# Five classes of experts instead of three, one slot table, alternating heavy and light experts, and rebuilt edges between the stages of a decoder layer

## The chip, the cores and the metric

The kernel runs on one core of one Trainium2 chip. The metric is the device time of one execution in microseconds (us). Lower is better.

## The reference

One layer of a hybrid decoder is computed for 1024 prompt tokens and 8 sample tokens (1032 in all, width 1024, everything in float32). Cut to what matters:

```
h = rms_norm(x);  q_lat | kv_lat | k_rope | conv_in | q_mem | gates = h @ w_in
y_a = latent attention (8 heads);  y_b = conv branch (GLU, depthwise conv of width 31, LayerNorm, silu)
y_c = cross-attention into 256 memory tokens (their keys and values come from rms_norm(mem) @ w_mem_kv)
x = x + (sig(g_a) * y_a + sig(g_b) * y_b + sig(g_c) * y_c) @ w_out
h = rms_norm(x)
scores = sigmoid(h @ w_router);  top 8 of 64 experts by scores + b_router, weights = scores / sum * 2.5
x = x + sum over chosen experts e of weight * (silu(h @ w_gate[e]) * (h @ w_up[e])) @ w_down[e]
      + (silu(h @ w_s_gate) * (h @ w_s_up)) @ w_s_down                        # shared expert
```

An expert has two matrices of 1024 x 256 and one of 256 x 1024, 3 MB in all. 1032 tokens with 8 choices each are 8256 (token, expert) pairs over 64 experts, 129 to an expert on average; the counts differ from expert to expert.

## The kernel before

The kernel is a row of stages with a barrier of all engines after each: `stage_constants`, `stage_front` (memory keys and values, normalised tokens), `stage_tokens` (prompt attention), `stage_sample` (sample attention), `stage_merge` (gates, branch projections, conv), `stage_mixer` (output projection, router, slot records, shared expert) and `stage_experts`. Inside a stage every engine has its own instruction stream, written out by hand, and waits on semaphores. SP issues most loads, and POOL issues the indirect transfers. Each engine works strictly in order.

**Constants and front.** `stage_constants` loads three tables and waits for them. `stage_front` then loads 11 row tiles; for each, ACT squares, POOL takes the root, DVE normalises, and PE transposes. DVE waits first for three small gain vectors (`gains_in`), one of them broadcast over the partitions (`gk`). PE works the memory projections in between, and at the end DVE normalises the memory keys.

**Merge.** PE makes gate columns (`gate`) and branch columns (`out`, needs the attention output `oT`) in units of 344 tokens; ACT takes sigmoids; DVE multiplies them (`merge`) and between them works 124 steps of the convolution (`conv`), 1024 columns each. POOL issues the loads of `oT` (`branch_in`) after the conv state has landed. Two banks hold the branch units, so PE can be at most two units ahead of DVE.

**Mixer.** For each of nine row tiles (the ninth is the 8 samples) PE projects with `w_out` (`project`), transposes the normalised rows (`turn`), makes router scores (`route`), and counts places (`rank`); DVE adds, normalises, takes the top 8 (`choose`), and works out the place of each slot record (`prefix`, `place`); POOL scatters the records (token and weight) to a table in DRAM. Six units of the shared expert (`shared`) fill PE at the end. `rank_experts` sorts the experts by count, so that rank 0 is the fullest.

**Experts.** Each rank has a fixed number of slots, its cap: `RANK_CAPS = ((192, 12), (160, 28), (128, 24))`. If a count is above the cap, the whole loop runs a second time over the next slots (`passes`). The experts are worked in order of rank. For an expert:

- SP loads the three matrices four experts ahead (`load`, rings of 4).
- POOL gathers the token rows as quarter rows, one indirect transfer for each 32 slots (`gather`, L2418), three experts ahead.
- DVE transposes them 32 x 32 (`turn`, L2524).
- PE multiplies gate and up (`gate_up`, L2612): 32 matmuls, moving columns = cap. ACT takes silu, DVE multiplies (`gate`, L2530).
- PE multiplies down (`down`): L2622 for the first 128 slots, L2630 for the tail (the slots beyond 128) in 2 or 4 column groups of the array.
- ACT (and DVE for half of the tail) scale the result by the slot weight into `yb`, two buffers.
- POOL adds the rows to the sums in DRAM by an indirect accumulating transfer: L2438 for the 128 rows, L2445 for the tail. Before each L2438 POOL waits until the adds of the expert before have landed (`added`), since two adds may touch the same row. The gathers three experts ahead stand before this wait in POOL's stream.

At the start of the loop PE also computes the down product of the shared expert (L2649), DVE adds it to x (L2542), and ACT stores the sums that the experts add to. After the loop SP copies the sums to the outputs.

Of the kernel before, what the change touches and what calls it, by code (L numbers as in the profile page):

```python
# [95 lines left out]
def stage_constants(nc, a, keep):  # L96

    with Core(nc) as c:
        loaded = c.sem("constants_loaded")
        cleared = c.sem("buffers_cleared")  # L100
        with c.block() as block:
            @block.sync
            def _(sp):
                sp.dma_start(keep.ident[:, :], a["k_ident"]).then_inc(loaded, 16)
                sp.dma_start(keep.cos[:, :, :], a["k_cos"].rearrange("(t p) c -> p t c", p=P)).then_inc(loaded, 16)
                sp.dma_start(keep.sin[:, :, :], a["k_sin"].rearrange("(t p) c -> p t c", p=P)).then_inc(loaded, 16)

                sp.wait_ge(loaded, 48)

            @block.gpsimd  # L110
            def _(pool):
                pool.memset(keep.mhalf[:, :], -0.5).then_inc(cleared, 1)
                pool.wait_ge(cleared, 1)


def stage_front(nc, a, o, keep):
# [4 lines left out]
    with Core(nc) as c:  # L121
# [19 lines left out]
        S = {n: c.sem("p_" + n) for n in """gains_in k_w_in v_w_in next_in squares mean rsq h_ready h_psum hT_ready k_psum v_psum k_out v_ready  # L141
# [20 lines left out]
        with c.block() as block:  # L162
            @block.sync
            def _(sp):
# [9 lines left out]
                rows(0)  # L174
                for dst, name in ((g_mem, "g_mem_norm"), (g_attn, "g_attn_norm")):
                    sp.dma_start(dst[:, :], a[name][0].rearrange("(k p) -> p k", p=P), allow_slow_non_contiguous=True).then_inc(S["gains_in"], 16)
                sp.dma_start(gk[:, :], a["g_k_mem"][0].partition_broadcast(P)).then_inc(S["gains_in"], 16)
# [7 lines left out]
                for j in range(9, ROWS_TILES):  # L185
                    rows(j)
                w_lat, w_qm, w_uq, w_uk, w_uv = keep.token_weights
# [15 lines left out]
                sp.wait_ge(S["next_in"], 112)  # L203
# [21 lines left out]
            def _(pool):  # L225
                for j in range(ROWS_TILES):
# [7 lines left out]
            def _(v):  # L234
# [16 lines left out]
                v.wait_ge(S["gains_in"], 48)  # L251
# [7 lines left out]
                v.wait_ge(S["k_out"], NMEM)  # L259
                v.tensor_tensor(kn[:, :], k[:, :], k[:, :], ALU.mult).then_inc(S["k_step"], 1)  # L260
                v.wait_ge(S["k_step"], 1)
                v.tensor_reduce(ssk[:, :], kn3, AX.X, ALU.add).then_inc(S["k_step"], 1)
                v.wait_ge(S["k_step"], 2)
                v.tensor_scalar(mnk[:, :], ssk[:, :], 1.0 / MHD, EPS, ALU.mult, ALU.add).then_inc(S["k_mean"], 1)
                v.wait_ge(S["k_rsq"], 1)
                v.tensor_tensor(kn3, k3, spread(rsk[:, :], MHD, 2), ALU.mult).then_inc(S["k_step"], 1)
                v.wait_ge(S["k_step"], 3)
                v.tensor_tensor(kn3, kn3, spread(gk[:, :], NMEM * MH), ALU.mult).then_inc(S["k_ready"], 1)

            @block.tensor  # L270
            def _(pe):
# [15 lines left out]

                for j in range(5):
                    turn(j)
# [1267 lines left out]
def stage_merge(nc, a, o, keep):  # L1557
# [8 lines left out]
    with Core(nc) as c:  # L1566
# [26 lines left out]
            last_psum last_ready stored state_moved""".split()}  # L1593
# [10 lines left out]
        with c.block() as block:  # L1604
            @block.sync
            def _(sp):
# [17 lines left out]

                def gated_rows(i):
# [6 lines left out]
                sp.dma_start(state, a["state_conv"][0].rearrange("(g b) r c -> (b r) g c", g=2)).then_inc(S["state_in"], 16)  # L1632
                gated_rows(0)
                weights(0, 0)
                weights(1, 0)
                for i in range(1, KC):
                    gated_rows(i)
                weights(2, 0)
                weights(3, 0)
                sp.dma_start(o["conv_s"][:, 0:HIST - 1, :], a["state_conv"][0][:, 1:HIST, :]).then_inc(S["state_moved"], 16)  # L1640
                for b in range(4, KD):
                    weights(b, 0)
# [1125 lines left out]
```

## Time and profile before

| | |
|---|---|
| median of 3 runs | 2620.87 us (2620.84 to 2622.55) |
| the profiled execution | 2621.16 us, its span 2619.3 us |
| PE busy | 2487.0 us (95%) |
| DVE, ACT, POOL busy | 1044.1, 594.9, 786.2 us |
| mean granted TensorE clock | 0.983 |
| bytes moved | 406.88 MB, 155 GB/s over the span |

The span is the time from the first to the last instruction. PE is TensorE's matmul stream, PEld its weight loads, DVE VectorE, ACT ScalarE, POOL GpSimd, SP SyncE; a q behind an engine's name is its sequencer, which issues transfers. A PE row counts two records for one float32 matmul. The stages in the trace: front to about 65 us, merge from 1116 to 1487, mixer from 1489 to 1717, experts from 1717 to the end.

### The profile page before, as it was taken

What the parts mean: (1) busy time and instruction counts of PE and PEld (TensorE: products, weight loads), DVE (VectorE), ACT (ScalarE), POOL (GpSimd) and SP (SyncE); (2) the same over time, 40 slices, a digit from 0 to 9 for tenths busy, and PEclk for the clock granted to TensorE, in tenths of its full rate; (3) what the DMA queues carried; (4) which work ended last, traced back from release to release, by engine and by line L of the source; (5) the groups of instructions that cost most, each with busy time, mean ns of one, the idle gap of its engine ahead of it and who ended that gap; (6) DMA issues with size and microseconds to landing.
All of it is one profiled execution on the core that took longest, in us unless ns stands there. A gap on an engine that the chain in (4) does not pass through costs nothing. (4 is left out here: it accounts for less than half of the span.)

```text
span 2619.3 us, 35201 instructions
## 1 busy us (share of the span) xinstructions
PE 2487.0 (95%) x12240; PEld 1665.7 (64%) x12240; DVE 1044.1 (40%) x2287; ACT 594.9 (23%) x1177; POOL 786.2 (30%) x590
## 2 busy tenths in 40 slices
PE   6999999999899999989999899889999999999995
PEld 3566666665645555556666655547777777787774
DVE  3223334544434444169952246433233333322220
ACT  2222333333233434110021111101112221121111
POOL 1000000000035455210000025435555666655542
PEclk9999999999899999999999999999999999999998
DMA  7111111010242221171112341077999999999996
GB/s 266 48 42 43 43 43 40 30 38 25 76 111 81 80 80 51 36 212 45 37 54 62 106 158 50 1 263 247 287 293 329 329 327 323 324 340 365 369 367 193
DMA packets 206451, 406.88 MB, mean 155 GB/s; under 512 B 55915, under 2 KB 135072, under 8 KB 189804
## 3 DMA queue, kind: packets, MB, share of 16 engines
q1 hardware_dynamic: 168884, 314.39, 34.9%
q0 software_dynamic: 29856, 78.51, 12.0%
q10 hardware_dynamic: 7536, 11.73, 1.2%
q8 instruction: 100, 1.64, 0.3%
q14 instruction: 75, 0.61, 0.1%
HBM read 343.53 MB, written 72.83 MB: 159 GB/s over the span
## 5 line engine op out<-in xcount | busy, mean ns | idle before, releaser
L2418 POOL DMA_INDIRECT mergedT<-tokens_normed,gather_rows x308 | 313.1, 1017 | 121.7 <-issue 96.6
L2612 PEld LDWEIGHTS pGe<-xT,we_g 128*128 128x128 f32 x2048 | 272.7, 191 | 46.6 <-issue 24.2
L2612 PE MATMUL pGe<-xT,we_g 128*128 128x160 f32 (+2 forms) x2048 | 286.0, 298 | 9.1 <-DVE xT L2524 9.0
L2612 PE MATMUL pUe<-xT,we_u 128*128 128x160 f32 (+2 forms) x2048 | 280.3, 295 | 0.0
L2612 PEld LDWEIGHTS pUe<-xT,we_u 128*128 128x128 f32 x2048 | 273.6, 191 | 0.0
L2524 DVE STREAM_TRANSPOSE xT<-mergedT 128x1280 f32<-128x1280 f32 (+2 forms) x64 | 154.3, 2412 | 266.0 <-DMA mergedT<-tokens_normed,gather_rows 266.0
L1403 PE MATMUL pKs<-ws_uk,cTs 128*128 128x512 f32 x512 | 234.4, 600 | 1.2 <-issue 1.2
L1116 POOL TENSOR_TENSOR rk<-ssk,half 128x32 f32<-128x32 f32 x32 | 173.3, 5427 | 191.7 <-DVE ssk L1245 191.7
L2622 PE MATMUL pYe<-we_d,h_e 128*128 128x512 f32 x512 | 230.1, 593 | 0.0
L2438 POOL DMA_INDIRECT sums<-mergedT,add_rows x64 | 103.9, 1624 | 269.5 <-issue 97.7
L2478 ACT ACTIVATE mergedT<-pYe,wc 128x512 f32<-128x512 f32 x128 | 88.0, 687 | 414.7 <-PE pYe L2622 414.7
L1313 DVE TENSOR_REDUCE ssk<-sqs 128x8 f32<-128x512 f32 x128 | 87.6, 684 | 210.4 <-ACT sqs L1179 210.1
L1727 DVE SCALAR_TENSOR_TENSOR y_conv<-hist,taps,y_conv 128x1024 f32<-128x1024 f32 x120 | 154.0, 1283 | 3.4
L1403 PEld LDWEIGHTS pKs<-ws_uk,cTs 128*128 128x128 f32 x512 | 92.5, 191 | 98.1 <-issue 97.1
L2622 PEld LDWEIGHTS pYe<-we_d,h_e 128*128 128x128 f32 x512 | 93.8, 191 | 92.2 <-issue 92.2
L1795 PE MATMUL pGate<-hT,branch_w 128*128 128x344 f32 x480 | 143.7, 453 | 0.0
L2221 PE MATMUL pXf<-w_out,mergedT 128*128 128x512 f32 (+2 forms) x320 | 128.9, 560 | 7.5 <-DMA w_out<-in_w_out 7.5
L1803 PE MATMUL pBranch<-oT,branch_w 128*128 128x344 f32 x384 | 120.1, 466 | 11.7 <-DMA oT<-attention_out 6.4
L499 POOL TENSOR_TENSOR r<-n,minus_half 128x16 f32<-128x16 f32 x9 | 26.1, 2899 | 328.5 <-DVE n L685 328.5
L808 PE MATMUL pFill<-hT,fill_w 128*128 128x344 f32 x384 | 119.9, 456 | 4.6 <-ACT fill_out L517 4.5
L808 PE MATMUL pFill<-hT,first_w 128*128 128x344 f32 x384 | 119.6, 457 | 2.5 <-ACT fill_out L517 2.5
L1795 PEld LDWEIGHTS pGate<-hT,branch_w 128*128 128x128 f32 x480 | 91.3, 190 | 47.3
(422 smaller groups left out, 3259.1 us busy)
## 6 DMA issues: line engine op xcount, KB each, us to landing
we_g<-in_w_e_gate SPq DMA_DIRECT2D x64, 1024.0 KB, 7.1
we_u<-in_w_e_up SPq DMA_DIRECT2D x64, 1024.0 KB, 11.7
we_d<-in_w_e_down SPq DMA_DIRECT2D x64, 1024.0 KB, 16.3
mergedT<-in_cache_latent SPq DMA_DIRECT2D x96, 128.0 KB, 2.1
raw_columns<-fill_out SPq DMA_DIRECT2D x48, 172.0 KB, 1.8
first_w<-in_w_in SPq DMA_DIRECT2D x12, 512.0 KB, 5.2
branch_w<-in_w_in SPq DMA_DIRECT2D x10, 512.0 KB, 4.8
mergedT<-tokens_normed,gather_rows POOLq DMA_INDIRECT x308
```

What stands on the lines that cost most here:

```text
L808: mm = pe.matmul(pG[:, 0:GN], ring[b % 2][:, k, :], keep.hT[:, k, g * GN:(g + 1) * GN], start=k == 0, stop=k == KD - 1)
L1116: pool.tensor_tensor(rk[b % 2][:, :, g, :], ssk[b % 2][:, :, g, :], half[:, :].rearrange("p (j h) -> p j h", h=NHEAD), ALU.pow).then_inc(S ...
L1403: mm = pe.matmul(pK[n % 2][:, :], cT[b % 2][:, k, n * P:(n + 1) * P], w_uk[:, k, :], start=k == 0, stop=k == KL - 1)
L1727: v.scalar_tensor_tensor(y[:, i, 0:SEQ], hist[:, i, j:j + SEQ], taps[:, i, j:j + 1], y[:, i, 0:SEQ], ALU.mult, ALU.add).then_inc(S["tap"], 1)
L1795: pe.matmul(pG[g][:, 0:n], ring[b % W][:, 4 + k, :] if b else keep.first_w[:, k, :], keep.hT[:, k, at:at + n], start=k == 0, stop=k == KD - 1)
L1803: mm = pe.matmul(pY[u % 2][:, 0:n], ring[b % W][:, k, :], branch[:, k, at:at + n], start=k == 0, stop=k == 3)
L2221: mm = pe.matmul(pX[p][0:r, at:at + n], keep.mergedT[:, k, cols_of(t)], w_out[:, k, at:at + n], start=k == 0, stop=k == KD - 1)
L2418: pool.indirect_dma_start(out=xg[v % 2][:, g, :], out_offset=None, in_=quarter, in_offset=bass.IndirectOffsetOnAxis(ap=gi[v % W][:, g:g + ...
L2438: pool.indirect_dma_start(out=keep.acc_dram[:, :], out_offset=bass.IndirectOffsetOnAxis(ap=si[u % W][:, 0:1], axis=0), in_=yb[u % 2][:, 0, ...
L2524: v.transpose(xT[p][:, :, 0:n * GR].rearrange("p c (g i) -> p g c i", g=n), xg[p][:, 0:n, :].rearrange("p g (j c) -> p g c j", c=KD)).then ...
L2612: mm = pe.matmul(dst[p][:, f * CAP:f * CAP + n], w[r][:, k, f * P:(f + 1) * P], xT[p][:, k, 0:n], start=k == 0, stop=k == KD - 1)
L2622: mm = pe.matmul(pY[half][:, :], h[p][:, f, 0:P], wd[r][:, f, half * 512:(half + 1) * 512], start=f == 0, stop=f == 1)
```

## The change

- `stage_constants` is gone. Its identity table is loaded in `stage_front` behind the first row tile, its cos and sin tables late in that stage, and `gk` after the row tiles with a semaphore of its own. DVE normalises the memory keys before it takes the last two transposed tiles.
- Merge: `branch_in` moves from POOL to SP. Its first half stands behind the weights of block 0 and the first raw conv rows; the other raw rows come between weight loads. ACT does the sigmoid of the first conv rows before the taps, DVE does 8 conv steps ahead of the first unit instead of 6, and the first 128 columns of `w_out` are loaded into `first_w` near the end of the stage.
- Mixer: the projection of tiles 0 and 1 begins with these 128 columns. The samples are projected in four column groups at once (`project_samples`). Shared units 0 to 3 stand between the last tiles' steps, and `rank(NTT - 2)` comes after `shared(2)`. `rank_experts` has five classes.
- Experts: `RANK_CAPS` has five classes, a pass is 128 slots further on, one table serves all classes, and the 28 experts of the lowest class are spread among the other 36. The first `turn` comes after the additions of seven tiles instead of five. At the end `down` of expert 62 comes before `gate_up` of expert 63, and silu and gate of 63 behind the scaling of 62.

```
-RANK_CAPS = ((192, 12), (160, 28), (128, 24))
-PASSES = max(-(-min(TOK, TOK * TOPK // (sum(n for _, n in RANK_CAPS[:i]) + 1)) // c) for i, (c, _) in enumerate(RANK_CAPS))
+RANK_CAPS = ((192, 4), (176, 8), (160, 8), (144, 16), (128, 28))
+PASSES = max(1 - (c - min(TOK, TOK * TOPK // (sum(n for _, n in RANK_CAPS[:i]) + 1))) // P for i, (c, _) in enumerate(RANK_CAPS))
+GT = P // GR * (PASSES - 1) + NG_E
...
-                    marks.mark(v.tensor_scalar(over[:, :], thr[0:NE, :], low, count, ALU.mult, ALU.is_lt))
+                    marks.mark(v.tensor_scalar(over[:, :], thr[0:NE, :], low, count, ALU.add, ALU.is_lt))
...
+    LIGHT = RANK_CAPS[-1][1]
+    ranks = {False: iter(range(NE - LIGHT)), True: iter(range(NE - LIGHT, NE))}
+    RANK_AT = [next(ranks[(u + 1) * LIGHT // NE > u * LIGHT // NE]) for u in range(NE)]
+    CAPS = [[c for c, n in RANK_CAPS for _ in range(n)][rank] for rank in RANK_AT]
+    GROUPS = [-(-c // GR) for c in CAPS]
...
-                                mm = pe.matmul(pZ[c * n:(c + 1) * n, 0:D // parts], h[p][:, f, P:P + n], wd[r][:, f, part(c, parts)], start=f == 0, stop=f == 1)
+                                mm = pe.matmul(pZ[P // parts * c:P // parts * c + n, 0:D // parts], h[p][:, f, P:P + n], wd[r][:, f, part(c, parts)], start=f == 0, stop=f == 1)
...
+                def project_samples():
+                    p = NT % 2
+                    pe.wait_ge(S["x2_ready"], NT - 1)
+                    for k in range(KD):
+                        for q in range(4):
+                            out = pX[p][32 * q:32 * q + DB, 0:256]
+                            x_k = keep.mergedT[:, k, SEQ:TOK]
+                            if q:
+                                mm = pe.matmul(out, x_k, w_out[:, k, q * 256 - P:(q + 1) * 256 - P], start=k == 0, stop=k == KD - 1)
+                            else:
+                                pe.matmul(out[:, 0:P], x_k, keep.first_w[:, k, :], start=k == 0, stop=k == KD - 1)
+                                pe.matmul(pX[p][0:DB, 512:512 + P], x_k, w_out[:, k, 0:P], start=k == 0, stop=k == KD - 1)
...
-                route(NTT - 1)
-                shared(1)
+                shared(2)
+                rank(NTT - 2)
+                route(NTT - 1)
+                shared(3)
...
-                pool.wait_ge(S["state_in"], 16)
-                branch_in(0)
```

## Rows read from the trace of the kernel before

**Rows 1.** Windows of the experts' loop: length, busy us by engine, clock, DMA share, GB/s.

```profile
1760.00:1945.00 185.00, 185.00 (x945) 145.99 (x944) 57.45 (x99) 27.86 (x44) 95.98 (x84) 1.00 0.86 280
1945.00:2340.00 395.00, 395.00 (x2616) 312.54 (x2613) 130.25 (x209) 80.39 (x146) 236.57 (x204) 1.00 1.01 326
2340.00:2562.00 222.00, 213.71 (x1439) 171.80 (x1438) 48.42 (x98) 35.14 (x60) 111.05 (x99) 1.00 1.03 364
```

**Rows 2.** Chain of waits, caps of 192, then of 160: start us, us, what.

```profile
1913.74 5.40 PE pGe L2612 x32
1924.34 3.43 PE pYe L2622 x8
1927.77 1.87 PE pZe L2630 x8
...
2039.68 4.54 PE pGe L2612 x32
...
2052.01 1.00 PE pZe L2630 x16
```

**Rows 3.** Timeline, an expert of cap 128: start us, us, engine, line, what.

```profile
2441.45 3.84 PE L2612 MATMUL pGe<-xT,we_g 128*128 128x128 f32 x32 [0.68 <-DVE xT L2524]
...
2448.70 3.60 PE L2622 MATMUL pYe<-we_d,h_e 128*128 128x512 f32 x8
```

**Rows 4.** Chain of waits later in the loop, the indirect adds.

```profile
2082.52 10.98 DMA sums<-mergedT,add_rows
...
2336.34 10.09 DMA sums<-mergedT,add_rows
...
2549.89 9.99 DMA sums<-mergedT,add_rows
```

**Rows 5.** The first adds (L2438) alone, landing time: 1780 to 1940, then 2340 to 2562.

```profile
DMA to landing us min/median/max: 8.4/10.8/11.7
...
DMA to landing us min/median/max: 10.0/10.1/10.9
```

**Rows 6.** Timeline, the front.

```profile
7.57 0.34 SPq L172 DMA_DIRECT2D mem_x<-in_mem_prompt  x1
15.89 0.15 DVE L238 TENSOR_SCALAR front_mean<-front_ss 128x1 f32<-128x1 f32 x1 [15.89 <-DMA mem_gk<-in_g_k_mem]
```

**Rows 7.** Timeline, the merge.

```profile
1132.66 1.23 DVE L1738 TENSOR_TENSOR hist<-convT,y_conv 128x1024 f32<-128x1024 f32 x1 [19.78 <-ACT y_conv L1676]
1140.55 8.84 PE L1803 MATMUL pBranch<-oT,branch_w 128*128 128x344 f32 x24 [6.35 <-DMA oT<-attention_out]
1145.42 0.51 DVE L1748 TENSOR_TENSOR mergedT<-gate_sig,pBranch 128x344 f32<-128x344 f32 x1 [3.91 <-ACT gate_sig L1694]
1305.40 4.93 PE L1803 MATMUL pBranch<-oT,branch_w 128*128 128x344 f32 x8 [4.77 <-DVE gated L1752]
```

**Rows 8.** Timeline, the mixer.

```profile
1494.63 29.87 PE L2221 MATMUL pXf<-w_out,mergedT 128*128 128x256 f32 x96 [7.45 <-DMA w_out<-in_w_out]
1626.31 7.03 PE L2221 MATMUL pXf<-w_out,mergedT 128*8 128x512 f32 x16
1652.91 0.69 PE L2251 MATMUL pCf<-chosen,before 128*128 128x64 f32 x2 [6.52 <-DVE chosen L2100]
1653.81 7.56 PE L2264 MATMUL pXf<-mergedT,w_sg 128*128 128x344 f32 x16
1661.21 4.79 PE L2264 MATMUL pXf<-mergedT,w_su 128*128 128x344 f32 x16
```

**Rows 9.** Timeline, the start of the experts' stage.

```profile
1751.25 3.76 PE L2649 MATMUL pZe<-w_sd,shared_hT 128*128 128x512 f32 x4 [6.06 <-DVE mergedT L2542]
1760.19 5.47 PE L2612 MATMUL pGe<-xT,we_g 128*128 128x192 f32 x32
```

**Rows 10.** Timeline, the end.

```profile
2584.01 7.03 PE L2622 MATMUL pYe<-we_d,h_e 128*128 128x512 f32 x16
2596.53 1.57 POOL L2438 DMA_INDIRECT sums<-mergedT,add_rows  x1 [5.77 <-DMA sums<-mergedT,add_rows]
```

More of the change, by code:

```diff
@@ L1929, in stage_mixer @@
         pR, pC = c.ps("pRf"), c.ps("pCf")
-        w_out_in = [c.sem(f"f_w_out_in{part}") for part in range(4)]
+        w_out_in = [c.sem(f"f_w_out_in{part}") for part in range(3)]
+        PARTS = ((P, 384), (384, 640), (640, D))
         x_in = [c.sem(f"f_x_in{p}") for p in range(2)]
@@ L1955, in x_load @@
                     sp.dma_start(x[t % 2][0:rows_of(t), :], src).then_inc(x_in[t % 2], 16)
-                for part in range(4):
-                    sp.dma_start(w_out[:, :, part * 256:(part + 1) * 256],
-                                 a["w_out"][0].rearrange("(k p) n -> p k n", p=P)[:, :, part * 256:(part + 1) * 256]).then_inc(w_out_in[part], 16)
+                for part, (at, end) in enumerate(PARTS):
+                    sp.dma_start(w_out[:, :, at - P:end - P], a["w_out"][0].rearrange("(k p) n -> p k n", p=P)[:, :, at:end]).then_inc(w_out_in[part], 16)
                 x_load(0)
@@ L2215, in project @@
                         pe.wait_ge(S["x2_ready"], t - 1)
-                    n = 512 if t else 256
-                    for at in range(half * 512, (half + 1) * 512, n):
-                        pe.wait_ge(w_out_in[at // 256], 16)
-                        pe.wait_ge(w_out_in[(at + n) // 256 - 1], 16)
+                    for at, end in pieces:
+                        for part, (first, past) in enumerate(PARTS):
+                            if at < past and first < end:
+                                pe.wait_ge(w_out_in[part], 16)
                         for k in range(KD):
-                            mm = pe.matmul(pX[p][0:r, at:at + n], keep.mergedT[:, k, cols_of(t)], w_out[:, k, at:at + n], start=k == 0, stop=k == KD - 1)
-                    if half:
+                            w = w_out[:, k, at - P:end - P] if at else keep.first_w[:, k, :]
+                            mm = pe.matmul(pX[p][0:r, at:end], keep.mergedT[:, k, cols_of(t)], w, start=k == 0, stop=k == KD - 1)
+                    if end == D:
                         mm.then_inc(S["x2_psum"], 1)
+                def project_samples():
[10 more added lines that the diff above has]
+                                pe.matmul(pX[p][0:DB, 512:512 + P], x_k, w_out[:, k, 0:P], start=k == 0, stop=k == KD - 1)
+                    mm.then_inc(S["x2_psum"], 1)
                 def turn(t):
@@ L2294, in stage_experts @@
     CQ = D // 4
-    CAPS = [c for c, n in RANK_CAPS for _ in range(n)]
-    NGS = sorted({c // GR for c in CAPS}, reverse=True)
+    LIGHT = RANK_CAPS[-1][1]
[3 more added lines that the diff above has]
+    GROUPS = [-(-c // GR) for c in CAPS]
+    RANK_CLASS = {c: i for i, (c, _) in enumerate(RANK_CAPS)}
     TAILS = sum(c > P for c in CAPS)
```

277 lines of the change are left out of this document (150 added, 127 removed).

## The prediction

> **What bounds the kernel now.** I read the slices of the page first: PE is busy in nine tenths of nearly every slice, so the first question is what work PE is given, and the second where its few pauses lie. For the experts' loop I then asked for windows [rows 1]: PE is busy for all of 1760 to 2340 and for 213.71 of the last 222 us, and at the same time the transfer engines are full, at 326 to 364 GB/s. The chain of waits shows which of the two ends last. Under cap 192 it is all PE, and an expert takes 15.90 us from its gate matmuls to the end of its tail (1913.74 to 1929.64); under cap 160 it is 13.33 us (2039.68 to 2053.01) [rows 2]. Later in the loop the chain runs through the indirect adds instead [rows 4]. From 2082.52 to 2336.34 it makes 19 steps, 13.36 us each, which is PE's own pace. From 2336.34 to 2549.89 it makes 19 steps of 11.24 us, where PE needs only 10.68: 7.25 us for gate and up [rows 3] and 3.43 for down [rows 2]. So there are two bounds close together: PE's work by cap, and POOL's rule that one expert's adds land before the next expert's start. An add takes about 10.1 us to land [rows 4, 5], so the next follows 1.1 us later; an expert with a tail has two adds, one behind the other, and takes 2.1 us more (13.36 less 11.24). The other stages are PE's, with pauses at the edges [rows 6 to 9]. After a pause PE is slow as well: 7.56 us for what takes 4.79 right behind it [rows 8].
>
> **The loop.** One step of 16 slots is half the difference between two caps. Gate and up take 15.90 - 3.43 - 1.87 = 10.60 us under cap 192 and 13.33 - 3.43 - 1.00 = 8.90 under 160 [rows 2], and 7.25 under 128 [rows 3]: 0.85 and 0.82 us a step. The tail of cap 176 keeps the two column groups of 512 columns (1.87), that of 144 the four groups of 256 (1.00), since the moving side is the same. So cap 176 takes 15.05 and cap 144 takes 12.50.
>
> - Before: 12 x 15.90 + 28 x 13.33 + 24 x 10.68 = 820.4 us. Measured, from the first gate matmul at 1760.19 [rows 9] to the last down at 2591.04 [rows 10], it is 830.9: the 10.5 more are mostly the light experts' wait for the adds (19 x 0.56 = 10.6 by rows 3 and 4).
> - After: 4 x 15.90 + 8 x 15.05 + 8 x 13.33 + 16 x 12.50 + 28 x 10.68 = 789.7 us.
>
> Now the second bound. Experts with a tail need about 13.3 us in the chain of adds (13.36 was PE-paced), light ones 11.24. With seven light to nine heavy, a heavy expert and its share of 0.78 light ones take: under 192 and 176, PE 24.2 and 23.4 against 22.1 in the chain, no loss; under 160, PE 21.7 against 22.1, a loss of 0.4; under 144, PE 20.8 against 22.1, a loss of 1.3. That is 8 x 0.4 + 16 x 1.3 = 24 us. Two things take from it. The adds may lag behind PE by some 5 us before the gathers, which stand behind them on POOL, come late; and a tail of 16 rows instead of 32 should land a little sooner, for which I take 0.2 us for 16 experts, 3 us. So the loss is 16 us, the loop 806, the gain 25. The ends of the loss are 0 (the chain never binds) and 27 us (neither lag nor shorter tails, and a few landings like the 10.98 of rows 4), so the gain lies between 14 and 41. By the caps there are 304 gathers against 308, and the weight loads stay. The extra DVE copy of a heavy expert lies in DVE's idle time (130 us busy of 395, rows 1).
>
> A rule of the Trainium skill bears on this. The first adds land in 10.8 us where the engines move 280 GB/s and in 10.1 us where they move 364 [rows 1, 5]. The page "DMA: Bandwidth & Descriptors" (Latency and other measured facts) says that lighter memory load makes the fixed cost of a transfer smaller. By that rule the mixed order would shorten the landings, since no stretch stays at 364 GB/s, and rival A would come; the trace has the opposite sign, so I leave its chance at 0.2.
>
> **The front.** The first row tile is requested at 7.57 us [rows 6], behind the constants block; now it is the first request, 6.8 us earlier. DVE's first step waited for the broadcast gains until 15.89, which is also gone, so behind it the loads of tiles and of memory weights are what is late. At the end the key stores leave before the last product: about 1 us. Gain 8, bounds 5 (loads take over) and 10.
>
> **The merge.** PE's wait of 6.35 us for `oT` goes, with about 1.9 us of slow clock: 24 records of 344 columns took 8.84, and by the 3.43 us for 8 of 512 [rows 2] they need 6.9 [rows 7]. SP's queue then holds 1.8 MB ahead of `oT` (state, weights, raw rows) and 2.1 MB of it; at the 326 GB/s of rows 1 that is 12 us from the stage's start at 1116, so it lands by about 1130, before PE asks at 1134.2 (1140.55 - 6.35). But DVE is next: at 1305.40 PE waits 4.77 us for it [rows 7], which then was behind with its conv steps. DVE starts about 3 us earlier (1132.66), loses the 3.91 us wait before 1145.42, and has two more conv steps of 1.3 us there: 3 + 3.9 - 2.6 = 4.3, and with part of the slow clock 5. Bounds 0 (ACT stuck behind the raw rows, which now hold up the taps) and 9 (DVE not binding).
>
> **The mixer.** PE's wait for `w_out` of 7.45 us [rows 8] takes in two projections of 128 columns, 16 matmuls, 3.84 us at full clock [rows 3]; I take 4.5, since part of the slow clock behind the wait falls into it too. A rule speaks against part of it: the page "TensorE: Matmul & The Clock Gate" (What's actually happening) says that the array starts at 1.2 GHz after idling. By it these projections take 7.7 us, which is more than the whole wait, and gain 3 at most; rows 8 show the same slowness behind the wait of 6.52. The samples cost two times 7.03 us [rows 8]; in four column groups 8 matmuls of 256 columns took 1.00 us [rows 2], and here are 32 such and 8 halves more: 4.0 to 4.9, against 14.1 if the groups do not overlap. I take 4.7: gain 9.4. The wait of 6.52 us before rank(7) goes behind shared(2), with the slow clock after it (7.56 - 4.79 = 2.8, and 0.6 in the rank products): 9.9. Splitting each projection at column 128 costs 0.2 us for 8 tiles, 1.5. The longer `rank_experts` (four classes more, about 2 us of small steps) lies under shared units 4 and 5, twice 4.79 us each [rows 8]; without this cover it would cost its 2 us. What is late next are the last tile's records on POOL: PE has only these two units, 19 us, left behind rank(8), and I expect both to end together. Sum 22, bounds 13 and 25.
>
> **Start and end of the experts.** PE waits 6.06 us for an addition that stands behind `turn` on DVE, and then runs slowly (3.76 for 4 records, half of the 3.43 for 8 in rows 2 is 1.7) [rows 9]. After the change the 16 records that are left at 1745.2 (1751.25 - 6.06) follow at once, 6.9 us, and PE reaches the first gate matmul at about 1752.1 instead of 1760.2; the one table costs 4 small DVE copies more, 0.5. Gain 7.5, bounds 3 and 9. At the end the last add waits 5.77 us for the one before [rows 10]. With expert 62's down first, that add starts 10.7 us earlier (7.25 + 3.43), and the last one follows the last product by about 2 us instead of 5.5 (2596.53 - 2591.04); PE now waits about 1 us for gate(63). Gain 2.5, bounds 0 and 5.
>
> **Sum.** 25 + 8 + 5 + 22 + 7.5 + 2.5 = 70 us against the profiled execution: 2621.16 - 70 = 2551.2. The median of the runs is 0.3 lower, so I predict 2551.
>
> **The rivals.**
>
> - A, the adds never bind: the loop is 790, the gain 41, the time 2551 - 16 = 2535. For it: under cap 192 PE was the only bound with landings as long. Against: in the light stretch they bound for 19 steps running. Chance 0.20.
> - B, the mixed order lengthens the chain of adds to 13.0 us on average (64 x 13.0 = 832), because the transfer engines were already full at 326 GB/s [rows 1] and the last third asks for about 350 (6.3 MB of weights and 2.1 of rows for a 144 and a 128 expert, in 24 us). The loop gains nothing: 2576. Against: the light stretch ran at 364 with the shortest landings. Chance 0.12.
> - C, slower: in the mixed order each expert, light or heavy, pays a heavy one's chain, since the gathers of a heavy expert and its tail hold POOL ahead of the light one's add. The place is POOL's stream, the price a step with the longest landing of rows 4, 14.2 us (10.98 + 2.1 + 1.1): 64 x 14.2 = 909, 103 more than forecast, 2654. It decides from a mean step of 13.7 on (the old loop's 830.9 and the 45 us gained outside it, over 64). Against: in the light stretch a step is its landing and 1.1 us, so the gathers lie inside the landing [rows 4]. Chance 0.03.
> - D, the change doesn't do what it says: a count above its cap makes a second pass, over 800 us. The reference's inputs with the default seed give counts, sorted, of 184, 164, 151, 139 and 125 at the first rank of each class, against 192, 176, 160, 144 and 128. Chance 0.01.
>
> **How the numbers follow.** The forecast has 0.64. Its own range, from the bounds of the loop and the edges taken together as independent, is 2534 to 2569. A is inside it; B lies 7 us above. I give 2530 to 2574, which leaves out C, D and the outer part of B. A difference under 0.2% (5.2 us) can't be told from none here. Forecast, A and B are faster: 0.95 with a little taken off for what I have not seen; C and D slower, 0.04; within 0.2%, 0.01.
>
> **What would show it.** The first tile's transfer at 1 us instead of 7.57. No wait of PE for `oT` or before rank(7). The samples' product at 4 to 5 us. Gate matmuls of 176 and 144 columns at the halves between their neighbours. In the last third of the loop, steps of about 24.0 to 24.6 us for a 144 and a 128 expert with the chain on the adds; 23.2 there means rival A, and 26 means B. It is wrong if the chain of waits leaves the adds and PE altogether, or if a stage outside the loop loses time.

## The result and the profile after

The changed kernel takes 2527.69 us (median of 4 runs, 2526.14 to 2532.28); the kernel before took 2621.48 beside it. The ratio is 0.9645, 95% interval 0.9628 to 0.9661: 93.8 us less, where 70 were forecast. The profiled execution is the longest of the four, 2532.28 us with a span of 2530.5, so against its own counterpart (2621.16) it shows 88.9 of them.

By the starts of the stages in the two traces, those 88.9 us are: front 9.8 (forecast 8), merge 6.1 (5), mixer 23.5 (22), start of the experts 1.3 (7.5), loop of the experts 43.5 (25), end 3.7 (2.5), and 0.9 between front and merge. Two terms are clearly off, with opposite signs: the loop gave 18.5 more and the start 6.2 less.

Windows of the experts' loop, columns as in [rows 1]:

```profile
1718.60:1830.00 111.40, 111.40 (x645) 91.36 (x645) 34.16 (x51) 16.39 (x27) 57.15 (x51) 1.00 0.89 302
1830.00:2000.00 170.00, 170.00 (x1000) 131.51 (x1000) 51.49 (x81) 28.85 (x47) 97.07 (x86) 1.00 1.01 333
2000.00:2160.00 160.00, 160.00 (x1073) 129.04 (x1072) 49.58 (x87) 29.76 (x53) 93.04 (x82) 1.00 1.03 353
2160.00:2480.00 320.00, 320.00 (x2223) 252.09 (x2222) 103.07 (x186) 64.17 (x115) 190.94 (x168) 1.00 1.03 359
```

PE is busy for every microsecond of the four. Before, it was busy for 213.71 of the last 222 us. The shares of the chain of waits that ended last, before and then after, have no DMA left, where before the adds of [rows 4] had 16% of the span:

```profile
DMA 17%; PE 12%; issue 3%; POOL 1%; POOLq 0%; DVE 0%; ACT 0%; DVEq 0%; ACTq 0%
PE 32%; DVE 0%; issue 0%; DVEq 0%; POOL 0%; ACT 0%; ACTq 0%; POOLq 0%
```

Timeline, one pair of a 144-slot and a 128-slot expert late in the loop; it answers to [rows 3]:

```profile
2455.08 4.19 PE L2644 MATMUL pGe<-xT,we_g 128*128 128x144 f32 x32
2459.10 4.08 PE L2644 MATMUL pUe<-xT,we_u 128*128 128x144 f32 x32
2463.02 3.60 PE L2654 MATMUL pYe<-we_d,first_w 128*128 128x512 f32 x8
2466.45 3.73 PE L2644 MATMUL pGe<-xT,we_g 128*128 128x128 f32 x32
2470.03 3.74 PE L2644 MATMUL pUe<-xT,we_u 128*128 128x128 f32 x32
2473.60 3.60 PE L2654 MATMUL pYe<-we_d,first_w 128*128 128x512 f32 x8
```

From 2455.08 to the next 144-slot expert at 2478.11 it is 23.03 us from start to start, all of it products: 7.15 + 3.43 for the light one, and 7.94 for gate and up, 3.53 for down and 0.98 for the tail of the other. The prediction named 24.0 to 24.6 here for itself and 23.2 for rival A. Rival A came.

The edges, one fence in order of time (front, merge, mixer, start of the experts, end); they answer to [rows 6 to 10]:

```profile
5.73 0.15 DVE L223 TENSOR_SCALAR front_mean<-front_ss 128x1 f32<-128x1 f32 x1 [5.73 <-DMA g_attn<-in_g_attn_norm]
55.52 4.77 PE L809 MATMUL pF<-w_lat,hT 128*128 128x288 f32 x13 [3.93 <-PEq L74]
...
1105.50 6.59 PE L1789 MATMUL pGate<-hT,first_w 128*128 128x344 f32 x16 [3.51 <-DVEq L1705]
1130.31 1.97 PE L1797 MATMUL pBranch<-oT,branch_w 128*128 128x344 f32 x6 [1.61 <-DVE mergedT L1742]
1288.98 3.78 PE L1797 MATMUL pBranch<-oT,branch_w 128*128 128x344 f32 x6 [4.88 <-DVE gated L1746]
...
1472.46 3.81 PE L2229 MATMUL pXf<-first_w,mergedT 128*128 128x128 f32 x32 [2.09 <-PEq L74]
1477.97 15.23 PE L2229 MATMUL pXf<-w_out,mergedT 128*128 128x256 f32 x72 [1.70 <-DMA w_out<-in_w_out]
1612.94 4.89 PE L2288 MATMUL pXf<-mergedT,w_sg 128*128 128x344 f32 x16
...
1680.30 6.75 PE L2685 MATMUL pYe<-w_sd,shared_hT 128*128 128x512 f32 x8 [5.06 <-issue]
1699.42 5.40 PE L2685 MATMUL pYe<-w_sd,shared_hT 128*128 128x512 f32 x8 [2.07 <-DVE mergedT L2577]
1712.33 2.94 DVE L2559 STREAM_TRANSPOSE xT<-mergedT 128x1536 f32<-128x1536 f32 x1
1718.58 3.68 PE L2644 MATMUL pGe<-xT,we_g 128*128 128x192 f32 x21
...
2502.19 3.69 PE L2654 MATMUL pYe<-we_d,first_w 128*128 128x512 f32 x8 [0.77 <-DVE first_w L2565]
2507.48 1.58 POOL L2465 DMA_INDIRECT sums<-mergedT,add_rows  x1 [5.97 <-ACT mergedT L2505]
```

The first step of DVE starts 10.2 us earlier. In the merge the wait of 6.35 us for `oT` is gone; in its place PE waits 1.61 us for DVE, and its later wait for DVE is still there, 4.88 against 4.77. In the mixer, where PE waited 7.45 us for `w_out`, stand the two 128-column projections, with 2.09 us of idling before them and 1.70 us of waiting behind. The samples' product runs from 1607.67 to 1612.94, 5.3 us. At the end the last add follows the end of the last product by 1.6 us instead of 5.5.

### The profile page after: what moved, and what is told of

It is laid out like the page before. It is cut to its first block and busy times, and to the rows that moved or that the text cites. A ratio compares the mean times of both kernels' runs of the same rounds, so it can differ in the third digit from the quotient of the medians.

```text
span 2530.5 us, 35418 instructions
## 1 busy us (share of the span) xinstructions
PE 2438.8 (96%) x12352; PEld 1645.8 (65%) x12352; DVE 1044.2 (41%) x2299; ACT 592.5 (23%) x1171; POOL 768.4 (30%) x574
## 5 line engine op out<-in xcount | busy, mean ns | idle before, releaser
L2644 PEld LDWEIGHTS pGe<-xT,we_g 128*128 128x128 f32 x2048 | 261.8, 191 | 33.2 <-issue 33.2
L2644 PE MATMUL pGe<-xT,we_g 128*128 128x128 f32 (+4 forms) x2048 | 270.8, 291 | 0.0
L2644 PE MATMUL pUe<-xT,we_u 128*128 128x128 f32 (+4 forms) x2048 | 267.0, 289 | 0.0
L2644 PEld LDWEIGHTS pUe<-xT,we_u 128*128 128x128 f32 x2048 | 260.7, 191 | 0.0
L2654 PE MATMUL pYe<-we_d,first_w 128*128 128x512 f32 x512 | 230.2, 593 | 0.8 <-DVE first_w L2565 0.8
L2654 PEld LDWEIGHTS pYe<-we_d,first_w 128*128 128x128 f32 x512 | 93.2, 190 | 93.3 <-issue 93.3
L1170 ACT ACTIVATE sqs<-pKs 128x512 f32<-128x512 f32 x128 | 76.2, 596 | 171.6 <-PE pKs L1394 170.1
```

The lines of the kernel that those rows point to most:

```text
L2644: mm = pe.matmul(dst[p][:, f * CAP:f * CAP + n], w[r][:, k, f * P:(f + 1) * P], xT[p][:, k, 0:n], start=k == 0, stop=k == KD - 1)
L2654: mm = pe.matmul(pY[half][:, :], h[p][:, f, 0:P], wd[r][:, f, half * 512:(half + 1) * 512], start=f == 0, stop=f == 1)
```

## The experiments

Twelve kernels ran, in four sets, on four chips. Four of them leave out work that the result needs (half of a product's depth, weight loads, or a share of the sums), and serve only to take a resource's load away. Each had the kernel before run beside it on its chip (its medians there: 2621.0 to 2622.4). Beside the medians I use one measure of the loop alone: the start of the first and of the last matmul of the down product, from the view of the tile `pYe`. Of before and after it reads:

```profile
L2622 PE MATMUL pYe<-we_d,h_e x512: 592/592/595, 1781.1 to 2590.5; 128*128 128x512 f32 x171
```

```profile
L2654 PE MATMUL pYe<-we_d,first_w x512: 592/592/692, 1739.5 to 2505.3; 128*128 128x512 f32 x171
```

809.4 and 765.8 us, a difference of 43.6.

| kernel | median, us | ratio to before, 95% | loop, us |
| --- | --- | --- | --- |
| before | 2621.0 to 2622.4 | 1 | 809.4 |
| three_rank_order | 2571.5 | 0.9809, 0.9792 to 0.9825 | 811.9 |
| three_alternating | 2559.8 | 0.9759, 0.9742 to 0.9775 | 797.6 |
| five_rank_order | 2545.3 | 0.9705, 0.9689 to 0.9721 | 782.9 |
| changed, again | 2527.7 | 0.9649, 0.9636 to 0.9662 | 765.9 |
| half_depth_rank_order | 2502.7 | 0.9542, 0.9522 to 0.9561 | 740.5 |
| light_without_down_loads | 2531.5 | 0.9650, 0.9634 to 0.9666 | 765.8 |
| adds_in_two_tables | 2544.0 | 0.9704, 0.9688 to 0.9720 | 780.3 |
| half_depth_without_loads | 2337.5 | 0.8913, 0.8896 to 0.8931 | 574.9 |
| warm_start_of_experts | 2530.8 | 0.9655, 0.9641 to 0.9668 | 765.8 |
| seven_classes | 2513.7 | 0.9587, 0.9574 to 0.9601 | 751.8 (-3.2) |
| eight_classes_with_112 | 2513.1 | 0.9596, 0.9583 to 0.9609 | 750.4 (-3.2) |
| old_turn_places | 2536.2 | 0.9671, 0.9658 to 0.9684 | 765.8 |

(-3.2: to be taken off for a comparison with the others, which have this much more ahead of their first down product; see below. In the two kernels of half depth less gate and up stands ahead of it too.)

### Classes and order apart

```diff
-    RANK_AT = [next(ranks[(u + 1) * LIGHT // NE > u * LIGHT // NE]) for u in range(NE)]
+    RANK_AT = list(range(NE))                                   # five_rank_order
-RANK_CAPS = ((192, 4), (176, 8), (160, 8), (144, 16), (128, 28))
+RANK_CAPS = ((192, 12), (160, 28), (128, 24))                   # three_alternating
                                                                 # three_rank_order: both
```

> The changed kernel (2527.7 us) with its experts in rank order again, largest class first, the 28 of 128 slots last; classes, table and all the rest as changed. In its profile a 128-slot expert costs TensorE 10.57 us (7.14 for gate and up, 3.43 for down), one of 144 slots 12.46. Theory 1: the chain of adds has a smallest step of 11.2 us for a 128-slot expert, as in the last third of the kernel before [rows 4], and one of about 11.7 us for an expert with a tail, under the 12.5 to 15.9 that TensorE takes for it; so only the stretch of 128-slot experts is held by it, 28 x 0.67 = 19 us less the slack at its start: about 2545 us. Theory 2, that of the prediction: an expert with a tail has a smallest step of 13.3 us, which also holds the sixteen of 144 slots (13.3 against 12.46): 19 + 13 = 32 us more, 2560. Theory 3: the adds hold nothing, the light stretch before was slow for another reason: within 4 us of 2528.

> The changed kernel with the three old classes (12 experts of 192 slots, 28 of 160, 24 of 128), heavy and light ones alternating. TensorE's sum by the prices of the changed kernel's profile: 12 x 15.9 + 28 x 13.3 + 24 x 10.57 = 817 us, against 786 for the five classes. Theory 1 (a tail expert's smallest step in the chain of adds is about 11.7): TensorE binds alone, 2527.7 + 31 = 2559. Theory 2 (13.3 for an expert with a tail, 11.2 for one without): the pairs of 160 and 128 slots are held at 24.5 instead of 23.9, 20 x 0.67 = 13 us more: 2572.

> The changed kernel with the three old classes in rank order: of the change only the edges of the stages and the one slot table are left. Its loop should take the 831 us of the kernel before, 44 more than the changed one: 2571 us by theories 1 and 2, so the edges are worth 50 us and the loop 44. Theory 3, under which the loop's 44 us come from somewhere else than classes and order (from the one table, or the start): clearly under 2565.

Measured 2545.3, 2559.8 and 2571.5 us, all within a microsecond of theory 1. The two halves of the loop's change nearly add up: with the order left as it was, five classes for three save 29.0 us of the loop (811.9 to 782.9); with the classes left, alternating saves 14.3 (811.9 to 797.6), and with five classes, which have 28 light experts for 24, it saves 17.1; both together 46.1. What is not classes or order is 2622.4 - 2571.5 = 51 us; only one of its edges was measured alone, the others are read from the traces. Theory 2, the prediction's 13.3 us for every expert with a tail, is out: it asked for 2560 and 2572 in the first two. That in rank order a light expert's step doesn't fall under 11.2 us stood so far, but not why.

### What a light expert's step is made of

```diff
-                            for k in range(KD):
+                            for k in range(KD // 2):       # gate and up, half_depth_rank_order
```

> Five classes in rank order, but the gate and up products sum over half of their depth (four of eight tiles), so TensorE needs only some 7 us for a 128-slot expert and 8.5 for one of 144: what is left of the loop is what the other resources allow, class by class. Loads, gathers, transposes and adds are all there. Theory 1: steps of 11.2 to 11.6 us for 128 slots and 11.5 to 12 for the classes with a tail: 36 x 11.8 + 28 x 11.3 = 741 us of loop, about 2485 in all. Theory 2: 13.3 for an expert with a tail: 36 x 13.3 + 28 x 11.3 = 795, about 2535. Theory 3 (neither adds nor memory near a limit): steps under 10.5 us, the whole under 2415.

The run took 2502.7 us. Its loop is 740.5 us, where theory 1 asked for 741 and theory 2 for 795; theory 1's total of 2485 was added up too low (741 and the 1762 us that the changed kernel has outside this stretch give 2503). With PE's work cut to 7.0 us for a light expert, the mean step from one first add to the next was 12.4 us under 160 slots, 11.9 under 144 and 11.3 under 128. The chain of waits at 128 slots still runs through the adds, and the transfer engines are at a share of 1.03. The window over its 128-slot experts, then the same stretch of five_rank_order, then one add in this run's chain:

```profile
2190.00:2450.00 260.00, 192.40 (x920) 140.36 (x920) 58.27 (x116) 40.46 (x69) 129.82 (x115) 0.88 1.03 365
```

```profile
2225.00:2495.00 270.00, 260.13 (x1737) 209.01 (x1736) 61.22 (x119) 42.18 (x72) 136.16 (x120) 0.99 1.03 366
```

```profile
2332.93 10.07 DMA sums<-mergedT,add_rows
```

Halving PE's work left rate and step as they were. That fits theory 1, and it also fits a new theory, M: a light expert moves 4.1 MB (98.9 MB for some 24 of them in the second window), and 4.1 MB at 365 GB/s is 11.3 us; the stretch is bound by memory traffic. Three runs were made to part it from the chain of adds.

```diff
                     for dst, name, sem in (...):
+                        if name == "w_e_down" and CAPS[u] == P: continue   # light_without_down_loads
+                        if u >= W: continue                                # half_depth_without_loads
...
-                    pool.wait_ge(added[0], 16 * (NE * q + u) + 16)         # adds_in_two_tables
-                    pool.wait_ge(added[1], 16 * (TAILS * q + tails(u)) + 16)
+                    wait_added(pool, q, u)                                 # only experts of u's parity
-                    pool.indirect_dma_start(out=keep.acc_dram[:, :], ...
+                    pool.indirect_dma_start(out=(keep.odd_dram if u % 2 else keep.acc_dram)[:, :], ...
```

> Five classes in rank order (2545.3 us, its 128-slot experts 11.3 us apart while TensorE needs 10.57 and idles 10 of 300 us; there the DMA engines' share is 1.02 and they move 361 GB/s), with one part left out: the 28 experts of 128 slots don't load their down weights (1 MB of the 4.1 MB that each moves) and use those of an earlier expert. Theory M, new after the half-depth run: memory traffic, not the chain of adds, paces that stretch (4.1 MB at 361 GB/s is 11.3 us); with 3.1 MB it is TensorE's 10.57 and the total falls by 18 to 20 us to 2526 or 2527. Theory 1 (the chain of waiting for an add, evicting and issuing the next has a smallest step of 11.2): still 2545, or a few us less if adds land sooner under a lighter load.

> Five classes in rank order, experts of odd place add into a second table of sums that is never read (their share is left out of the result), so an add waits only for the one two experts before it, and ScalarE and VectorE wait for that one alone. The bytes are the same. Theory M: the stretch of 128-slot experts stays at 11.3 us a step and the total within 3 us of 2545. Theory 1: its smallest step is gone, 10.57 a step, about 2527.

> The half-depth kernel in rank order (2502.7 us; steps of 12.7 to 11.6 us with a tail, 11.3 without, DMA share 1.03), with one more part left out: only the first four experts load weights, the others reuse them. Gathers and the chain of adds are all there. Theory M: the chain's own smallest step is far below what it seemed: 128-slot experts go at TensorE's 7.0 us or at GpSimd's issue of four gathers and an add (4 x 1.3 + 1.9 = 7.1), those with a tail at GpSimd's 5 x 1.3 + 1.9 + 1.8 = 10.2 (six gathers 11.5) or less: the total under 2390. Theory 1: 11.2 and 11.6 as before, total within 15 us of 2502. Theory 2 of the prediction (13.3 with a tail) is already contradicted by the half-depth run's 11.6 to 12.7.

The three took 2531.5, 2544.0 and 2337.5 us. Their windows over their light experts, in this order:

```profile
2220.00:2490.00 270.00, 270.00 (x1849) 222.02 (x1848) 75.09 (x126) 44.31 (x76) 144.73 (x127) 1.00 0.96 286
```

```profile
2220.00:2490.00 270.00, 260.71 (x1742) 208.32 (x1741) 69.22 (x124) 42.54 (x73) 138.15 (x122) 1.00 1.03 364
```

```profile
2130.00:2300.00 170.00, 165.24 (x900) 113.56 (x899) 60.96 (x113) 40.36 (x69) 126.68 (x112) 1.00 0.64 129
```

What PE waits for in the light stretch, in five_rank_order (2225 to 2495) and in adds_in_two_tables (2220 to 2490), as us in total, times and longest, and a piece of the latter's chain of waits:

```profile
PE pGe L2644 <- DVE xT L2559: 9.7, 10, 2.9
```

```profile
PE pGe L2652 <- DMA we_u<-in_w_e_up: 9.3, 12, 1.7
...
2380.05 21.70 DMA we_u<-in_w_e_up
```

With a quarter of a light expert's bytes gone, PE is busy for all of 270 us and the loop takes 765.8 us, to the tenth what alternating gives (the total is 4 to 5 us over theory M's, because this profiled execution reached its first gate matmul 6.3 us later than that of five_rank_order). This run alone doesn't part the theories: its chain of adds has the same waits, but an add also lands sooner when less is moved. In the stretch of 128-slot experts single steps between two adds go down to 7.6 us (2276.16 to 2283.80), where in five_rank_order none is under 10.6 (the last three, behind which nothing is gathered, apart).

adds_in_two_tables parts them. With the chain loosened and the bytes kept, PE still idles 9.3 of 270 us, the engines move 364 GB/s, and the total stays (2544.0 against 2545.3). No add waits for an add there any more; PE, which in five_rank_order waited for rows whose gathers stand behind the adds, now waits for weights that SP had asked for 21.7 us before. The loop is 2.6 us shorter of the 17 that alternating gives, so the chain of adds is at most a small part of it. Theory M holds, and theory 1 falls as a reason, though the adds do stand in the chain of waits in rank order: their 10.1 us shrink when less is moved.

Without loads the chain shows how short it can be. POOL's timeline there, first for a 128-slot expert, then for one of 144, and a piece of the chain of waits:

```profile
2204.88 1.64 POOL L2467 DMA_INDIRECT sums<-mergedT,add_rows  x1 [0.42 <-issue]
2206.82 1.04 POOL L2447 DMA_INDIRECT mergedT<-tokens_normed,gather_rows  x1 [0.31 <-issue]
...
2212.10 1.63 POOL L2467 DMA_INDIRECT sums<-mergedT,add_rows  x1 [0.33 <-issue]
...
2029.22 1.64 POOL L2467 DMA_INDIRECT sums<-mergedT,add_rows  x1 [0.31 <-issue]
...
2039.43 1.64 POOL L2467 DMA_INDIRECT sums<-mergedT,add_rows  x1 [0.30 <-issue]
...
2029.22 6.07 DMA sums<-mergedT,add_rows
```

A light expert takes 7.2 us and is paced by POOL's own issue (four gathers 1.30 us apart and an add of 1.94); one of 144 slots takes 10.2 (2029.22 to 2039.43), five gathers and two adds. Both are what theory M named. The first add issued at 2029.22 landed after 6.1 us at 116 GB/s, where the one of the half-depth run above took 10.1 at 365. So the chain's step is no constant: the landings stretch with the traffic.

### Where the gain of finer classes ends

```diff
-RANK_CAPS = ((192, 4), (176, 8), (160, 8), (144, 16), (128, 28))
+RANK_CAPS = ((192, 2), (176, 2), (168, 6), (160, 4), (152, 3), (144, 13), (128, 34))             # seven_classes
+RANK_CAPS = ((192, 2), (176, 2), (168, 6), (160, 4), (152, 3), (144, 13), (128, 21), (112, 13))  # eight_classes_with_112
```

> The changed kernel itself once more, beside the next three on one chip, so that differences of 2 to 4 us can be told: 2527.7 us within 3, with runs from 2526 to 2532 as at its first measurement.

> The changed kernel with seven classes closer to this input's counts, alternating: 2 experts of 192, 2 of 176, 6 of 168, 4 of 160, 3 of 152, 13 of 144, 34 of 128 slots: 9064 slots in place of 9344, 280 x 0.056 = 15.6 us less of gate and up, and six tails of 1.0 us less: 21.6 us. Theory M: the loop's 265 MB at 361 GB/s need 735 us, TensorE's sum is still above it at 766: the whole gain arrives, 2506. Rival (theory 1 or 2, a chain with a smallest step of 11.2 and more): mean step 11.97 is at or under the chain's 11.2 to 11.8 for a mixture, and about half the gain arrives: 2515 or more.

> As the seven classes, with 13 of the 128-slot experts at 112 slots (this holds only while none of them has more than 112 tokens, as with this input): 13 x 16 x 0.056 = 11.6 us less for TensorE, whose sum is then 755 us. The bytes stay as they are. Theory M: the memory's 735 us are near but under it; between 2494 (all of the gain) and 2500. If the total stays at that of the seven classes (2506), memory is the limit already at 766.

The changed kernel came out at 2527.66 us again. Seven classes take 2513.7 us, 13.9 less by the medians of the same chip, and beat both kernels; 21.6 were expected. That lies between theory M's 2506 and the rival's 2515, nearer to the rival. Eight take 2513.1, and what they should have taken from PE on top did not come off at all. The down products start to start make 14.1 and 15.5 us less than the changed kernel's 765.9, but their second expert is a light one, with 3.2 us less of gate and up ahead of the first down; from the first gate matmul the seven classes' loop is 17.2 us shorter. Another 3.5 us of the missing gain lie ahead of the loop, which the profiled execution reached at 1718.0 us, and changed_again at 1714.5. PE's timeline of the seven classes at 2179, and DVE's beside it:

```profile
2179.08 1.06 PE L2662 MATMUL pZe<-we_d,first_w 128*16 128x256 f32 x16
2182.83 5.86 PE L2644 MATMUL pGe<-xT,we_g 128*128 128x144 f32 x32 [2.69 <-DVE xT L2559]
```

```profile
2180.32 2.46 DVE L2559 STREAM_TRANSPOSE xT<-mergedT 128x1280 f32<-128x1280 f32 x1 [12.85 <-DMA mergedT<-tokens_normed,gather_rows]
```

Here PE stands for rows that are still being gathered: 2.7 us of waiting and 1.8 of slow matmuls behind it, with smaller ones later, some 4 us in all. The window from 2030 to 2440 shows PE just short of full, and the transfer engines at a share of 1.03:

```profile
2030.00:2440.00 410.00, 406.60 (x2786) 325.13 (x2786) 122.97 (x226) 77.01 (x137) 238.35 (x208) 1.00 1.03 360
```

PE's sum and the traffic have come close together: M's 735 us were 265 MB over 361 GB/s, a mean that left no room for an uneven demand. Whether memory or the chain of adds held these rows isn't shown. The chain of waits there runs through the adds again, with landings of 8.7 to 10.6 us, and no run took bytes or waits out of this kernel. The eight classes' timeline, a 112-slot expert and the light class beside it in the same kernel's groups:

```profile
2387.66 3.72 PE L2644 MATMUL pGe<-xT,we_g 128*128 128x112 f32 x32
2391.22 3.74 PE L2644 MATMUL pUe<-xT,we_u 128*128 128x112 f32 x32
```

3.56 us from the one to the next, where 128 slots take 3.57: 16 columns fewer save nothing. My 0.056 us a slot, read between 128 and 192, does not go on there, so this run says nothing on memory. The seven classes leave margins down to one slot on this input (127 tokens in 128); an input with more in any class pays a second pass.

### The start of the experts

```diff
                 pe.matmul(pC[0:1, NE:2 * NE], ...).then_inc(S["ranked"], 1)
+                for i in range(6):                        # warm_start_of_experts
+                    pe.matmul(pT[:, 0:512], keep.ident[:, :], keep.mergedT[:, 0, 0:512], start=i == 0, stop=i == 5)
...
-                    for t in range(2, 7): add(t)
-                    turn(q, 0)
-                    for t in range(7, NTT): add(t)
-                    turn(q, 1)
+                    add 2 to 4, turn 0, add 5 and 6, turn 1, add 7 and 8      # old_turn_places
```

> The changed kernel with six more products of 128 x 512 at the end of TensorE's work in the mixer, results not used, 6 x 0.43 = 2.6 us. In the changed kernel TensorE idles 5.06 us there and the first eight matmuls of the shared down product then take 6.75 us instead of 3.70 (one matmul 1217 ns instead of 592), where the kernel before idled 3.61 us and its first eight took 3.70 [rows 9]. Theory A: the idle stretch before it costs the clock; with the idle under 3.6 us the first group takes 3.70, and later ones that follow a wait of 2 us too: 3 us faster if the stage's end waits for something else, about nothing gained if TensorE itself is the last to reach it (the barrier then moves by 2.6 us). Theory B: the slow matmuls have another cause: the first group stays at 6.7 us, and the total is 0 to 2.6 us slower.

> The changed kernel (2527.7 us) with one edge undone: at the start of the experts VectorE takes the transposes of the first two experts after five and seven tiles of sums, as before, and not after seven and nine. Theory S (the new places do save the stall of the kernel before, 6.06 us of TensorE behind a VectorE that waits 8.64 us for the gathers; what was gained so was given back ahead of it, by a stage border 1.5 us longer and by matmuls at the low clock): the stall comes back, 5 to 6 us slower, about 2533. Theory G (the places are worth nothing now, because the gathers land before VectorE asks for them; this is why the stage's start gained only 1.3 us instead of 7.5): within 1.5 us of 2527.7.

old_turn_places, PE and DVE:

```profile
1709.31 2.92 DVE L2559 STREAM_TRANSPOSE xT<-mergedT 128x1536 f32<-128x1536 f32 x1 [8.27 <-DMA mergedT<-tokens_normed,gather_rows]
1712.86 3.78 PE L2687 MATMUL pZe<-w_sd,shared_hT 128*128 128x512 f32 x4 [5.67 <-DVE mergedT L2577]
```

The stall of [rows 9] is back, 5.67 us against 6.06, with the slow matmuls behind it, and the total is 8.5 us longer (by the ratios to before 0.9671 - 0.9649, 5.8 us). Theory S holds: the new places save what was forecast. What gave it back lies in front of them. The clock column tells it; the first matmuls of the shared down product, after and before:

```profile
1680.30:1687.00 6.70, 6.70 (x9) 2.82 (x10) 0.69 (x1) 0.00 (x0) 2.41 (x3) 0.54 0.69 177
```

```profile
1719.00:1723.00 4.00, 3.84 (x9) 1.82 (x10) 0.80 (x2) 0.00 (x0) 2.55 (x4) 1.00 0.67 94
```

PE idles 5.06 us at the stage's border instead of 3.61 (1.5 us), and then has 0.54 of its clock granted, most of it at the lower of the two levels (1.2 GHz), where it had 2.4: 6.75 us for eight records instead of 3.70 (3.0 us). A second such group, 5.40 at 1699.42 (clock 0.70), costs 1.7 more. Together 6.2, the whole of the miss. That is the profiled execution, the slowest of its four. In the profile of changed_again the first group took 5.66 us and the second 3.70, and from the end of the mixer's products to the first gate matmul it is 40.7 us, against 43.6 in the first profile and 44.9 before: there the start gained 4.2 us and not 1.3. The warm start did not cure it, and theory A's condition was met:

```profile
1674.57 5.42 PE L2320 MATMUL pTf<-mergedT,ident 128*128 128x512 f32 x12
1682.39 5.39 PE L2687 MATMUL pYe<-w_sd,shared_hT 128*128 128x512 f32 x8 [2.41 <-issue]
```

The six products took 5.4 us, twice what I had put, at full clock (one product is two records of 0.45), the border moved back with them, so PE itself is the last to reach it, and after only 2.41 us of idling the first group still took 5.39. By the medians it is 3.1 us slower, by the ratios 1.6, which five runs hardly tell from nothing. So theory A is out as it stood: the idle stretch at the border doesn't decide the clock by its length. 5.1 us and 2.4 us were followed by the low clock, 3.6 us before the change and 2.1 us in front of the mixer were not, and behind 2.0 to 2.3 us at the second group the clock fell in four of the thirteen profiles with the new edges, all four with a first group of 6.6 us or more, and stayed in the nine others. What decides it stays open.

## Why the prediction was wrong in size

The direction held, and four of the six terms were near; the time came out 23 us lower than forecast. Point by point:

- **PE's sum.** 789.7 us were forecast and 787.3 measured. The halves between the classes are right (12.45 us for an expert of 144 slots, 12.50 forecast); the light expert's 10.68 was read behind a wait of 0.68 us, where the gate product took 0.1 us more, and is 10.58. The mechanism, less work for the engine that sets the loop, was right: the classes alone took 29 us from the loop, the order 14 to 17.
- **The second bound.** This is the step that failed, as the prediction put it: "Experts with a tail need about 13.3 us in the chain of adds (13.36 was PE-paced), light ones 11.24." The first number was PE's own pace, as the bracket says, and was used as the chain's all the same. In the half-depth run the experts of 160 and 144 slots went at 12.4 and 11.9, without loads those of 144 at 10.2. The second number was real, but it is no smallest step of the chain: it is 4.1 MB at 365 GB/s, and it went when the bytes went and stayed when the chain was loosened. So the loss of 16 us, which made 806 of 790, is 0. Alternating did not lengthen the chain of a pair; it spread the light experts' demand for memory (more than 365 GB/s at PE's pace: 4.1 MB in 10.57 us is 388) over heavy neighbours that ask for less (by the last window's 115 MB, an estimate, some 4.2 MB in 12.5 us, 335), with four weight buffers to carry them; that the buffers are what evens it out was argued and not tested. The row that could have raised the question was there: the light stretch was the only one at 364 GB/s [rows 1].
- **Rival A** named the outcome, 790 for the loop. It had 0.20. That the adds hold nothing is true in the mixed order, where PE has no wait in the four windows; but it gave no reason why they should stop holding, and in rank order they do stand in the chain. **Rival B** had the right resource, the transfer engines, and the wrong rate: it took 326 GB/s for full, where 359 is moved in the last third. Its own argument against, the stretch at 364, was the better one.
- **The rule on landings.** The prediction held a rule of the Trainium skill to be of the opposite sign to the trace: the page "DMA: Bandwidth & Descriptors" (Latency and other measured facts) says that a lighter memory load makes a transfer's fixed cost smaller. Over a wider range the runs agree with its sign: a first add landed in 6.1 us at 116 GB/s and in 10.1 at 365. They show whole landings and not the fixed part. Between 280 and 364 GB/s, where the prediction looked, the landings moved the other way by 0.7 us, and no run shows why.
- **Front, merge, mixer, end.** 9.8, 6.1, 23.5 and 3.7 for 8, 5, 22 and 2.5. `oT` is no longer waited for and DVE is next, as forecast. The samples took 5.3 us for 4.7, at a clock of 0.55 for most of it. The two projections took 3.81 us at full clock after 2.09 us of idling. The 1.2 GHz that the Trainium skill's page "TensorE: Matmul & The Clock Gate" (What's actually happening) states for an array that has idled didn't show there; it did at the start of the experts, after 5.06 us.
- **Start of the experts.** Forecast 7.5, got 1.3. The stall went as worked out (old_turn_places brings it back); I had priced nothing for the border ahead of it, and its 1.5 us and 4.7 us of low clock ate the gain in the profiled execution; in the second profile they took less (4.2 us gained).

## What to carry to other kernels

A step time read from a stretch is the pace of whatever is slowest there; before it is used as the smallest step of a chain, look whether another resource may be full in the same stretch. The share of the transfer engines raises that question and doesn't settle it: it is 1.03 in the changed kernel too, where PE never waits, and 0.96 with a quarter of the bytes gone. Nor does the chain of waits: it named the adds. What settled it was to loosen the suspected chain with the other resource's load left as it was, and to see whether the total moved and what was waited for instead. A stretch that is short of memory bandwidth and one that is short of TensorE can be mixed, and then sums count and not stretches: here that cost nothing at a mean step of 12.3 us, and some 4 us with seven classes. And the pause at a stage's border is worth a term of its own, together with the clock behind it.

## What the hardware showed beside that

A product of 112 columns takes as long as one of 128, 3.56 against 3.57 us for 32 records, while 144 take 4.02 (each record with new weights).

The transfer engines' share has no fixed price per byte. Queues of the changed kernel, 2160 to 2480 us, then of half_depth_without_loads, 2130 to 2300 (packets, MB, share of 16 engines):

```profile
q1 hardware_dynamic: 15303, 85.79, 67.2%
q0 software_dynamic: 10495, 28.82, 35.5%
...
q0 software_dynamic: 7624, 21.69, 63.4%
```

In the first, the indirect gathers and adds (q0) took 1.23% of the engines' time per MB and the weight loads (q1) 0.78%, 1.57 times less. But the same kind of row transfers with no loads beside them took more, not less: 63.4% of 170 us for 21.69 MB is 5.0 us per MB, against 3.9 (35.5% of 320 us for 28.82). So the share holds waiting as well as moving, and the factor of 1.57 is that of this stretch. At the start of the experts' stage, from 1705 to 1718 us, the engines moved 412 GB/s at a share of 1.02, with gathers, loads and stores but no adds among them.
